# Expert rows gathered head by head: v rows mixed among u rows from the 44th on, and both of the first two tiles' rows all taken in the second half of the prompt

## The reference, cut to what matters

```
q = (h @ peer_wq).reshape(n, PEER_HEADS, 2, PEER_HALF)
s = einsum('nhcd,hckd->nhck', q, peer_sub_keys)
...
best_s, best_pos = lax.top_k(cand_s, PEER_TOPK)
experts = jnp.take_along_axis(cand_i, best_pos, axis=-1)
g = jax.nn.softmax(best_s, axis=-1)
act = jax.nn.gelu(jnp.einsum('nd,nhkd->nhk', h, peer_u[experts]))
return jnp.einsum('nhk,nhkd->nd', g * act, peer_v[experts])
```

## Time and profile before

| | |
|---|---|
| median of 3 runs | 2813.51 us (2808.73 to 2839.88) |
| the profiled execution, its own time | 2817.09 us |
| its span in the trace | 2815.3 us |
| busy: PE, DVE, ACT, POOL | 74%, 52%, 24%, 53% |
| moved by DMA | 843.32 MB, mean 300 GB/s |
| TensorE's mean granted clock | 0.851 |

### The profile page before, as it was taken

The page is one execution under the profiler, slowest core; times in us unless marked ns, Lnnn a source line. Parts: engine busy times, 40 slices in busy tenths (PEclk is TensorE's granted clock), DMA queues, the critical chain, the costliest instruction groups (busy, mean ns, idle before and its releaser), DMA issues. The chain is left out here.

```text
span 2815.3 us, 31629 instructions
## 1 busy us (share of the span) xinstructions
PE 2074.6 (74%) x10995; PEld 1316.1 (47%) x10995; DVE 1453.5 (52%) x3506; ACT 673.1 (24%) x2035; POOL 1485.4 (53%) x1493
## 2 busy tenths in 40 slices
PE   8999989987977989988989846753377775653045
PEld 6788865665655657644454623331244442110011
DVE  3321023146998966446621757868765663015800
ACT  5431026123556210025521122310111110000000
POOL 1120000025556865646554877777776676657765
PEclk9999989988988999989989967856588897777568
DMA  5224454446886999979799789999999999999998
GB/s 177 104 75 144 141 222 153 173 144 212 306 302 194 408 379 357 368 264 338 278 353 401 276 310 388 407 348 344 383 349 383 377 369 360 403 386 379 345 361 316
DMA packets 209780, 843.32 MB, mean 300 GB/s; under 512 B 25752, under 2 KB 32728, under 8 KB 190104
## 3 DMA queue, kind: packets, MB, share of 16 engines
q0 software_dynamic: 170912, 644.95, 61.1%
q1 hardware_dynamic: 38712, 196.36, 18.8%
HBM read 821.80 MB, written 23.54 MB: 300 GB/s over the span
## 5 line engine op out<-in xcount | busy, mean ns | idle before, releaser
L3604 POOL DMA_INDIRECT e_ring<-in_peer_u,e_idx x523 | 620.9, 1187 | 339.5 <-DVE e_dot L3768 176.9
L3768 DVE CUSTOM_DVE_ANT_0 e_ring<-e_ring,e_h 128x1024 f32<-128x1024 f32 x523 | 630.0, 1241 | 66.2 <-issue 24.5
L3604 POOL DMA_INDIRECT e_ring<-in_peer_v,e_idxT x487 | 505.2, 1037 | 288.7 <-issue 132.3
L3671 PE MATMUL ps<-e_ring,e_wz 128*32 128x512 f32 x1948 | 327.9, 703 | 240.6 <-issue 114.3
L3671 PEld LDWEIGHTS ps<-e_ring,e_wz 128*32 128x32 f32 x1948 | 71.7, 120 | 404.6 <-issue 391.7
L363 PE MATMUL ps<-hT_ahead,wb 128*128 128x320 f32 x384 | 110.9, 444 | 0.6 <-DMA wb<-in_weights 0.6
L363 PEld LDWEIGHTS ps<-hT_ahead,wb 128*128 128x128 f32 x384 | 73.1, 195 | 29.9 <-issue 2.9
L1815 POOL CAST ra_atf<-ra_at 128x32 f32<-128x32 uint32 x8 | 1.7, 210 | 150.7 <-DVE ra_hit L1808 150.7
L3812 DVE TENSOR_TENSOR e_x<-e_x,ps 128x512 f32<-128x512 f32 x10 | 6.4, 684 | 143.3 <-PE ps L3671 78.8
L1180 POOL MEMSET inda<- 128x256 f32 x1 | 0.3, 311 | 147.7 <-POOLq L4071 147.7
L3671 PE MATMUL ps<-ring_pair,e_wz 128*32 128x512 f32 x152 | 64.6, 747 | 14.3 <-DMA e_ring<-in_peer_v,e_idxT 10.8
(11 more groups left out here) (778 smaller groups left out, 4715.2 us busy)
## 6 DMA issues: line engine op xcount, KB each, us to landing
wb<-in_weights SPq DMA_DIRECT2D x65, 1024.0 KB, 4.9
e_ring<-in_weights SPq DMA_DIRECT2D x36, 1024.0 KB, 4.9
wb<-in_late_weights SPq DMA_DIRECT2D x6, 2048.0 KB, 10.1
room<-in_late_weights SPq DMA_DIRECT2D x6, 2048.0 KB, 14.9
h<-in_weights SPq DMA_DIRECT2D x10, 1024.0 KB
xs<-in_weights SPq DMA_DIRECT2D x9, 1024.0 KB
e_ring<-in_peer_u,e_idx POOLq DMA_INDIRECT x523
e_ring<-in_peer_v,e_idxT POOLq DMA_INDIRECT x487
```

The source lines that it names most:

```text
L3604: nc.gpsimd.indirect_dma_start(out=self.room(place), out_offset=None, in_=k.peer_u if kind == "u" else k.peer_v, in_offset=off).then_inc(s ...
L3671: last = nc.tensor.matmul(k.ps[32 * b:32 * b + 32, self.SUMS + i, :], self.wz[:, at:at + 32], self.room(self.v_at[n])[:, 512 * i:512 * i + ...
L3768: v.tensor_tensor_reduce(uu, uu, self.h[:, tile % 2, :], 1.0, 0.0, ALU.mult, ALU.add, self.dot[:, tile % 2, t:t + 1]).then_inc(self.dotted, 1)
```

## The change

**A finer routing.** A step is now one head of one tile: 16 u gathers. Its gelu, `weigh`, `turn`, `stage_v` and `fill` run 36 times in all (8 for each of four tiles, 4 for tile 4) where the first four ran 5 times. A v gather now takes the 16 picks of one head for 8 tokens. `weigh` becomes three DVE instructions (one of 128x16, two of 128x128), `turn` two matmuls of 16 columns, `stage_v` two copies of 16 columns, and `fill` moves from ACT to DVE as one instruction over 512 elements. In return v gathers of head 0 can stand right behind u gathers of head 0.

**Another order.** `weave` mixes groups of four v gathers among groups of four u gathers, as evenly as it can. Tile 0's first 44 u gathers stand alone; from there u and v alternate in a ratio of 212 to 168 until tile 1's last u gather, and then the 88 v gathers left of the two tiles follow. All 512 places of the first two tiles thus stand ahead of tile 2's first u gather (448 places before, so that 64 v gathers of tile 1 stood behind it). Tiles 2 and 3 are laid the same way: 44 u gathers alone, then one v for each u.

**Other shares.** In the second half they become conv 72 (60), ssd 44 (28), zgate 62 (56), bs 52 (46), cmp_prompt 14 (10), attn_prompt 108 (100), ba 36 (30), query 52 (46): 512 in place of 448. The sample's shares stay as written, but `plan` cuts them at the first u gather of tile 4, which now stands at place 980 (996 before). The stages ahead come to 512 + 440 = 952, sample_out then gets 28 of its 32, and sample_query 0 of its 76. What is left for `rest` is 172 places (156 before).

| places, of them u / v | before | now |
|---|---|---|
| conv | 60 / 0 | 60 / 12 |
| ssd | 28 / 0 | 28 / 16 |
| zgate | 56 / 0 | 32 / 30 |
| bs | 30 / 16 | 30 / 22 |
| attn_prompt | 52 / 48 | 60 / 48 |
| ba, out, query | 0 / 96 | 8 / 100 |
| state | 72 / 40 | 80 / 32 |
| sample_query | 0 / 76 | 0 / 0 |

Ranking of tile 1's heads begins at place 60 with a step of 24 (20 and 30 before). In the attention stage `turn` shares a PSUM bank with the gate matmuls, so it waits for their copy and they wait for it. POOL builds three small masks in the first stage. x1 and y move with one DMA in place of four.

```diff
+            for mask, per in ((ex.by_eight, 8), (ex.by_topk, TOPK)):
...
+            for a in range(P // 8):
+                own(gp.affine_select(out=ex.in_eight[:], in_=ex.in_eight[:], compare_op=ALU.not_equal, fill=1.0, base=-8 * a,
+                                     pattern=[[-1, 8]], channel_multiplier=1))
...
+                if lo == 0 and ex.turn_count:
+                    pe.wait_ge(ex.routed_v, ex.turn_count)
...
-        LAG, LATE = 28, 64
...
+        START, BEFORE, HERE = 44, 168, 2 * P
+        us, vs = list(range(T)), list(range(T))
+        u(0, 0, START)
+        weave(us[START:2 * P], vs[0:BEFORE])
+        for n in range(BEFORE, HERE, 4):
+            v(n // P, n % P, n % P + 4)
+        weave(us[2 * P:2 * P + START], vs[HERE:2 * P])
+        weave(us[2 * P + START:4 * P], vs[2 * P:4 * P - START])
+        weave(us[4 * P:], vs[4 * P - START:4 * P])
+        for n in range(4 * P, T, 4):
+            v(n // P, n % P, n % P + 4)
...
+                put("act", last + 4, lambda s=s: self.gelu(s))
+                ready = max(last + 6, routed[t] + 3, turn + 1)
+                turn = self.turn_place(ready + 5)
+                put("dve", ready, lambda s=s: self.weigh(s))
+                put("pe", turn, lambda s=s: self.turn(s))
+                turn = max(turn + 1, self.turn_place(turn, 1))
+                put("act", turn, lambda s=s: self.stage_v(s))
+                used = self.v_at[P * t + TOPK * h]
+                fill = max(turn + 2, self.v_at[self.before(P * t + TOPK * h, 2) + TOPK - 4] + 6 if s >= 2 else 0)
+                assert fill + 5 < used and turn + self.NR < used, (s, last, turn, fill, used)
+                put("dve", fill, lambda s=s: self.fill(s))
...
-        if kind == "v" and t == 0:
-            pool.wait_ge(self.routed_v, tile + 1)
+        if kind == "v" and t % TOPK == 0:
+            pool.wait_ge(self.routed_v, n // TOPK + 1)
...
+        if self.shared:
+            pe.wait_ge(*self.shared)
...
+        act.wait_ge(self.dotted, TOPK * (s + 1))
...
+        self.own(v.tensor_tensor(d, d, self.of_step(self.rw, s), ALU.mult))
...
+        v.tensor_tensor(self.wide_w[:], over(d), own_eighth, ALU.mult)
+        v.tensor_tensor(self.wide_idx[:], over(self.of_step(self.named, s)), own_eighth, ALU.mult).then_inc(self.weighed, 1)
...
+        v.tensor_tensor(room.rearrange("p r (b y) -> p r b y", y=32)[:, :, :, 0:8], w, own_topk,
+                        ALU.mult).then_inc(self.filled, 1)
...
-    k.share = dict(norm=0, conv=60, ssd=28, zgate=56, bs=46, kv=22, qk=30, cmp_prompt=10, attn_prompt=100, ba=30, out=20, query=46,
+    k.share = dict(norm=0, conv=72, ssd=44, zgate=62, bs=52, kv=22, qk=30, cmp_prompt=14, attn_prompt=108, ba=36, out=20, query=52,
```

More of the change, by code:

```diff
@@ L3464, in lay_out @@
         put("pool", 0, lambda: self.load_x1(0))
-        turns = [self.u_at[P * t + self.ups(t) - 1] + 3 for t in range(TILES)]
-        assert not any(turn <= place <= turn + 1 for turn in turns for place in squares.values())
-        self.squares_before = [sum(place < turn for place in squares.values()) for turn in turns]
-        for j in range(T // self.FILL):
-            n = self.FILL * j
-            tile = n // P
-            routed = self.u_at[P * tile + self.ups(tile) - 1] + 5
-            put("act", max(self.v_at[max(n - 4, 0)], routed) if j else self.v_at[0] - 4, lambda j=j: self.fill(j))
         for p, (kind, n) in enumerate(order):
@@ L3478, in lay_out, with before, turn_place @@
         self.steps, self.end = steps, 2 * T + 32
+    def before(self, n, steps):
+        return n - TOPK * steps
+    def turn_place(self, place, past=0):
+        lo, hi = self.spread
+        if lo <= place < hi:
+            hooks = 2 * 2 * HPK
+            at = lambda i: lo + (hi - lo) * i // hooks
+            i = next(i for i in range(hooks) if at(i + 1) > place)
+            return at(i - i % 4 + 3 + past) if i % 4 != 3 or past else place
+        return place
     def rank_place(self, t, step):
         if t == 0 and step >= 0:
-            return 20 + 30 * (step // 9) + step % 9
+            return 60 + 24 * (step // 9) + step % 9
         return self.u_at[P * t + 20 + step]
@@ L3621, in load_scores @@
             self.s_in[count % 2], 16)
-    def quarters(self, dram, tile):
-        return dram.rearrange("(q b) d -> b q d", b=4), rows(tile) // 4
     def store_y(self, tile):
```

218 lines of the change are left out of this document (110 added, 108 removed).

## The result

The changed kernel takes 2859.93 us in the median of four runs (2853.00 to 2867.12), the kernel before 2820.35 us beside it: a ratio of 1.013, 95% interval 1.009 to 1.017. It is slower by about 40 us where the forecast said 4 us less, and it lies above the forecast's range. Its profiled execution took 2865.49 us, its span is 2863.5 us.

A forecast was written before the change was run, and what follows sets the result against it. The prediction took the kernel as bound by gathers from 671 us on, except where another stage's chain holds them up. Terms 2 + 44 + 2 - 52 = -4 us on 2817.1 gave 2813, median 2809.5, range 2768 to 2850.

The forecast's parts named there:

- the prediction's own signs of being wrong: Attn_prompt or ssd growing by over 20 us, or the second half growing by less than 25 us.
- The second half, stage by stage, +44 us: Conv to query: 64 more gathers lengthen these stages by 44 us, summed from terms for each stage.
- it can win only by filling the 93 us: Idle DMA time in the stages shown, 93 us, is the only gain, since no byte fewer is moved.
- Eight matmuls at 168 ns each: Zgate: a v sum on PE costs 1.35 us, so 7.5 sums add 10 us; the stage's term is +9.
- State ... DVE busy 152 of 190: 94%, +5: State: 8 dots, one ranked head and five steps more, about 27 us of DVE work, lengthen it by 5 us.
- In mix and sbs ... -5: Mix and sbs: a run of u gathers alone becomes an even mix, saving 5 us.
- in attn ... +2: The sample's attention: only 8 us of steps on DVE are added, costing 2 us.
- Sample_query and rest, -52 us: The end: routing 72 us and rest 228 against 359, -59; ring drain ahead +12; fewer gathers in sample_out -5.
- The first stage: Start of the kernel: POOL's 23 small new instructions end just past the block, costing 2 us (bounds 0 and 6).
- Chains pay for the steps: Rival, conv, ssd and attn_prompt: engines wait for each other in each step; half exposed adds 35 us, 2845; chance 0.2.
- The holes take nearly everything: Rival: the second half grows only by its three full stages, 24 us, and sample_query drains in 5; 2782; chance 0.27.
- Routing comes late for the gathers: Rival: POOL waits for each head's routing at a step's first v gather; 10 us at each gives 2830; chance 0.05.

The follow-up runs named there:

- f1: The kernel before, unchanged, run again for its trace on the second group's chip: 2823.07 us.
- f2: The changed kernel itself, run beside the kernel before on the second group's chip: 2855.26 us, ratio 1.0125.
- g2: Routing by heads alone, with places, order and shares of the kernel before, on the third group's chip: 2844.84 us, ratio 1.0072 to the kernel before.
- g4: The changed kernel with the old shares (448 places in the second half) and 128 instead of 168 v rows mixed in: 2874.84 us, ratio 1.0193 to before.
- e1: Routing by heads alone, with order, ranking places and shares of the kernel before, on the first group's chip: 2782.35 us, ratio 1.0164 to before.
- f4: The kernel before plus the routing steps' work, done into scratch without their waits between engines: 2835.50 us, ratio 1.0063 to before.
- g1: The kernel before, unchanged, run again for its trace on the third group's chip: 2815.76 us.
- e4: The changed kernel with more places between a head's last dot and its gelu, weighing and transposition: 2783.73 us, ratio 1.0177 to before.
- h4: The changed kernel itself, run on the fourth group's faster chip: 2793.07 us, ratio 1.0162 to the kernel before.
- h3: Four column groups as in h1, plus 64 v rows held back to stand ahead of the sample's u rows: 2784.38 us, 0.994 of h1.
- h1: The changed kernel with the sample's v sums in four of TensorE's column groups again instead of two: 2800.66 us, ratio 1.0183 to before.
- e3: The changed kernel with fewer places in the sample's earlier stages, so that 60 fall to sample_query: 2793.18 us, ratio 1.0208 to before.
- e2: The changed kernel with a plain copy in place of the gelu, so no table is loaded for it: 2774.44 us, ratio 1.0146 to before.
- i1: The kernel before with 6 of conv's 60 places moved to the query stage: 2819.76 us, ratio 0.9993 to before.
- i2: The kernel before with conv 50 (60), zgate 60 (56), attn_prompt 98 (100), ba 28 (30), query 56 (46): 2815.67 us, ratio 0.9975 to before.

## Why the prediction was wrong

Its sum was -4 us; the profiled executions differ by 48.2 us (2863.5 less 2815.3), those of f1 and f2 by 30.6, and the medians of the result by 40. Both pairs miss in the second half, by 19 and 18 us more than forecast. In the stages up to sample_query, forecast at +2, the first pair has +30.5 and the second +9; at the end, forecast at -52, they have -52 and -41. None of the prediction's own signs of being wrong came; but ssd's DMA share, told as above 0.85, was 0.74.

Where does the loss come from? Routing by heads, order and shares were taken apart on chips of like speed: by heads alone 1.0072 (g2), with the new order 1.0193 (g4), with the shares too 1.0125 (f2). So the routing costs some 0.7% (on another chip 1.6%, e1), the order some 1.2% more, and the shares, from which the forecast took its gain, do win 0.7% back. The forecast had no term for either of the first two beyond the steps' work: for the new order it had +5 in state and -5 in mix and sbs and the hole, and g4 loses without a hole.

**"The second half, stage by stage, +44 us".** Measured +63, and +62 in f2 against f1. This is the step that failed in both pairs. Its base was "it can win only by filling the 93 us": the holes were taken as room. 64 gathers more, 84 us of transfer, were to make the half 44 us longer, so 40 us were to vanish in idle DMA time. They took 15 us off it in the first pair (130 to 115), 24 in the second and 32 against g4, and cost 0.85 us each (f2 against g4). That a gather's dot (1.25 us of DVE) or sum is what keeps a hole from being filled is the likely reason, not a tested one. Term by term: conv +17 (and +20) for "+5", of which g2 gives 10 to the steps at unchanged places (f4: 3 of them as work), while DVE, forecast to fall, went from 113.91 to 119.03 us and 6.6 us of sums on PE had no price; ssd +9.5 for "+5"; ba +11.5 (and +13) for "+7", cmp_prompt +5 for "+1", out +5 for "0". Right were zgate (+9 for "+9", PE busy 78.26 to 90.01) and, in the first pair, attn_prompt (+7 for "+8"; -6 in f2, so the term is not known to better than that). Bs gave -1 for "+7".

**"Eight matmuls at 168 ns each".** A sum has sixteen in the rows that the 168 ns come from. At that mean they would take 2.7 us; in zgate they overlap more, 13.82 us for 116 or 1.9 us a sum, not 1.35. The term for zgate came out right by two errors; the one for conv was missing.

**"State ... DVE busy 152 of 190: 94%, +5".** The work was right, 27 us more on DVE (152.06 to 178.87). The price was wrong: the forecast let 22 of the 27 us vanish in DVE's idle time, and state grew by 19.5 us (17 in f2). The steps alone don't do it: state is 194 us in g1 and in g2, 193 in f4, and 204 in g4, so it comes with the new order. The gelu's wait for its dots is not the cause either: in e4 it shrinks to 3 us, and state is 203 us all the same, as in h4. That wait in state, first in the changed kernel (1710:1920), then in e4 (1690:1893):

```profile
ACT e_dot L3718 <- DVE e_dot L3795: 24.7, 4, 11.5
ACT e_dot L3718 <- DVE e_dot L3795: 3.1, 2, 1.7
```

**"In mix and sbs ... -5", "in attn ... +2".** Mix, sbs, cmp, the attention and the branch stage behind it came to +11 in the first pair and to -8 in f2: their sum is not told from the terms by these traces.

**"Sample_query and rest, -52 us".** Measured -52 in the first pair (sample_out -17, the rest -35), -41 in f2. Its parts were less right: the routing took 77 us for "72", with 19 gathers for "16" and DMA at 0.67 for "0.65"; the rest took 246 us for "228", with 154 gathers for "156", or 1.6 us a gather with refill and tail where the forecast's sum comes to 1.46; in exchange "drain +12" and "-5" were -17. So that the first pair meets -52 is luck: two errors of some 23 us cancel. The first head was named 41 us after the weights' issue, as said.

**The first stage, "+2 us"**: the second half began 6.5 us later in the first pair, and at the same time in f2.

**The rivals.** "Chains pay for the steps" had the direction and most of the amount (2845). f4 prices the work at 1.0063, g2 the work with its waits at 1.0072, with intervals of 0.3 to 0.4% on either side; so on chips of that speed the waits between engines, on which that rival rested, show no price of their own. What e1's 1.0164 is made of is not known, and the new order's part of the loss is not in that rival. The hole in sample_query is worth some 16 us (h3 against h1) if it is filled by another order; filled by other shares it wins nothing (e3, g4). "The holes take nearly everything" is refuted: the second half grew by 63 us, 54 of them with the places (f2 against g4), not by 24. "Routing comes late for the gathers": POOL's waits in the changed kernel have none for a head's routing, only the 40.1 us for the naming of tile 4's first head. e4, which makes the routing later still, is no test of it in time. The loads of the gelu's table cost some thousandths (e2). The drain that the Trainium skill states (ScalarE: Activation LUTs, What ACT_TABLE_LOAD costs) is not seen in the trace: of the changed kernel's 91 loads, 58 have ACT's next instruction starting within 12 ns behind them, and 51 of these have the one before ending within 19 ns ahead as well.

**What stays open.** What in the new order costs 1.2% was not found; g4 shows only where, in state and the stages behind it. Routing by heads raises the idle DMA time of the sample's part from 65 to 93 us at the same bytes (g2, whose profiled execution was its longest), f4's work to 68 only. So that loss is waiting, but no single wait was found for it. Why the sums fell behind near the end on the slower chips, and not on the faster ones, is open too, and so is e1's 1.0164 against g2's 1.0072.

## What to carry to other kernels

Idle DMA time in a stage is not room by itself: here 64 gathers more took 15 to 32 us off it and lengthened the stages by 54. Price a moved gather with the work behind it (a dot on DVE, a sum on PE). A list of prices by stage, read from one pair of traces, is a guess until a run has moved a few gathers by it: here i1 and i2 did, and stages whose places had not changed moved by up to 16 us. Take routing, order and shares apart before the prediction is summed; each may have a price of its own, and a change that joins them can lose by one what it wins by another. When an order is rewritten, ask at each point where routing must come first how many transfers are still free to be issued (in the same 77 us 18 gathers were issued in h1 and 41 in h3). A count in a sum (matmuls for one row) is checked in the rows before it is multiplied.

## What the runs showed of the hardware

Sums into four column groups of PE ran side by side, sixteen 128x512 matmuls in 1.72 us back to back (g1); into two groups the same sixteen took 3.43 us (f2), both at a granted clock of 1.00. At the pace of the transfers this didn't matter (h1).

POOL issues a gather every 1.24 us at best (1.235 us is the least from start to start in any trace of this case); the transfer of its 524 KB takes 1.28 us at the 411 GB/s of ba, the highest rate in the stages shown. Timeline of POOL in the changed kernel:

```profile
2591.99 0.94 POOL L3640 DMA_INDIRECT e_ring<-in_peer_v,e_idxT  x1 [0.30 <-issue]
```

The same two kernels stood at 1.0164 on one chip (e1) and 1.0072 on another (g2): a difference of one per cent can belong to the chip.
